# Normalising a block by token halves in a single-core transformer stack

## The reference, cut to what matters

```
def _rmsnorm(x, g):
    x32 = x.astype(jnp.float32)
    y = x32 * lax.rsqrt(jnp.mean(x32 * x32, axis=-1, keepdims=True) + RMS_EPS)
    return (y * g.astype(jnp.float32)).astype(x.dtype)
...
        u = _rmsnorm(h, norm_g[i, 0]) * (1 + sc1) + sh1
        h = h + MACARON_WEIGHT * g1 * _swiglu(u, ffn_w_gate[i, 0], ffn_w_up[i, 0], ffn_w_down[i, 0])
        u = _rmsnorm(h, norm_g[i, 1]) * (1 + sc2) + sh2
...
            mix = _hybrid_mixer(u, positions, hyb_w_in[j], fox_b_f[j], hyb_w_out[j])
...
            mix = _mla_mixer(u, positions, mla_w_down[j], mla_q_norm[j], mla_kv_norm[j],
                             mla_w_uq[j], mla_w_ukv[j], mla_w_out[j])
        h = h + g2 * mix
```

## Time and profile before

| | before |
|---|---|
| median of 3 runs | 3476.15 us |
| span of the profiled execution | 3472.8 us |
| around the span, against the median | 3.35 us |
| TensorE (PE) busy | 3406.4 us, 98% of the span |
| VectorE (DVE) busy | 2199.6 us, 63% |
| ScalarE (ACT) busy | 600.3 us, 17% |
| mean granted TensorE clock | 0.996 |

### The profile page before, as it was taken

How to read it: one execution, slowest core, us unless ns; L and a number is a source line. 1 busy time by engine, 2 the same in 40 slices (tenths; PEclk the granted TensorE clock), 3 DMA queues, 4 the chain that set the end, 5 groups by cost and what they waited for, 6 DMA issues and landing times.

```text
span 3472.8 us, 40732 instructions
## 1 busy us (share of the span) xinstructions
PE 3406.4 (98%) x16336; PEld 2811.9 (81%) x16336; DVE 2199.6 (63%) x4356; ACT 600.3 (17%) x1260; POOL 10.6 (0%) x12
## 2 busy tenths in 40 slices
PE   8999999999999999999999999999999999999999
PEld 6888867768888888888578888877688866888888
DVE  7776858767767677565356545554346567677754
ACT  2000023331000010001331000023411244012100
POOL 0000000000000000000000000010000000000000
PEclk9999999999999999999999999999999999999999
DMA  6433412213434434332112222222222211222222
GB/s 254 156 135 141 181 64 88 91 41 127 149 122 159 164 140 153 112 114 83 51 49 74 94 87 79 91 87 70 67 75 85 84 67 61 85 80 91 85 79 79
DMA packets 62083, 355.72 MB, mean 102 GB/s; under 512 B 6292, under 2 KB 15124, under 8 KB 32276
## 3 DMA queue, kind: packets, MB, share of 16 engines
q1 hardware_dynamic: 61895, 353.12, 29.2%
HBM read 350.83 MB, written 9.34 MB: 104 GB/s over the span
## 4 chain that ended last, share of the span: by engine, by line
PE 87%; DVE 9%; issue 2%; DMA 1%; ACT 1%; DVEq 0%; SPq 0%; ACTq 0%
PE turn L424 37%; PE lin L424 29%; PE lin L366 4%; PE lin L476 4%; PE turn L366 3%; PE score L1435 2%; PE out L1464 1%; PE lin L473 1%; DMA normed_T<-in_ada 1%; DVE work L823 1%; PE turn L1449 1%; PE out L424 1%; DVE work L2888 1%; DVE normed_sums L567 1%; PE turn L476 1%
## 5 line engine op out<-in xcount | busy, mean ns | idle before, releaser
L424 PE MATMUL turn<-normed_sums,weight_ring 128*128 128x256 f32 x3712 | 867.6, 379 | 0.4 <-DVE small L2907 0.4
L424 PEld LDWEIGHTS turn<-normed_sums,weight_ring 128*128 128x128 f32 x3712 | 705.0, 190 | 96.8 <-DVE small L2907 0.8
L424 PE MATMUL lin<-normed_T,weight_ring 128*128 128x256 f32 x2096 | 479.9, 380 | 1.2 <-ACT normed_T L779 1.2
L424 PEld LDWEIGHTS lin<-normed_T,weight_ring 128*128 128x128 f32 x2096 | 397.6, 190 | 58.8 <-issue 5.2
L503 DVE TENSOR_TENSOR products<-products,lin 128x512 f32<-128x512 f32 x182 | 125.1, 687 | 406.9 <-PE lin L424 378.8
L424 PE MATMUL turn<-arena,weight_ring 128*128 128x256 f32 x1618 | 371.3, 379 | 0.6 <-DVE arena L567 0.6
L424 PE MATMUL lin<-arena,weight_ring 128*128 128x256 f32 x1608 | 364.7, 380 | 2.0 <-DVE weight_ring L535 1.6
L424 PE MATMUL lin<-normed_sums,weight_ring 128*128 128x256 f32 x1432 | 345.5, 380 | 4.1 <-DVE normed_sums L567 4.1
L424 PEld LDWEIGHTS lin<-arena,weight_ring 128*128 128x128 f32 x1608 | 304.4, 190 | 45.8 <-DVE weight_ring L535 3.3
L424 PEld LDWEIGHTS turn<-arena,weight_ring 128*128 128x128 f32 x1618 | 306.6, 190 | 42.3 <-issue 1.0
L424 PEld LDWEIGHTS lin<-normed_sums,weight_ring 128*128 128x128 f32 x1432 | 270.9, 190 | 44.1 <-issue 6.2
(11 more groups left out here) (329 smaller groups left out, 3363.4 us busy)
## 6 DMA issues: line engine op xcount, KB each, us to landing
weight_ring<-in_up SPq DMA_DIRECT2D x110, 1024.0 KB, 4.8
arena<-in_ada SPq DMA_DIRECT2D x54, 768.0 KB, 4.4
weight_ring<-in_down SPq DMA_DIRECT2D x40, 1024.0 KB, 5.0
normed_T<-in_ada SPq DMA_DIRECT2D x36, 768.0 KB, 4.6
weight_ring<-in_down SPq DMA_DIRECT2D x20, 768.0 KB, 4.3
weight_ring<-in_dil_qk SPq DMA_DIRECT2D x9, 1024.0 KB, 5.0
weight_ring<-in_hyb_qk SPq DMA_DIRECT2D x8, 1024.0 KB, 4.8
weight_ring<-in_xbc SPq DMA_DIRECT2D x6, 1024.0 KB, 5.0
```

The costliest lines, as they stand in the source:

```text
L424: last = pe.matmul(o[:, n * H:(n + 1) * H], weight_block(slot, pairs, block, kp), op(kind, kp0 + kp), start=opens and n == 0 and kp == kps ...
```

## The change

Before, a norm treats all 512 tokens at once; after, it treats tokens 0 to 255 and then tokens 256 to 511. In the last slab of a stage the groups go a, b, c, e, d: c is now t3 alone, and d is t1 and b22, the two products that only the second token half needs. In a down projection this holds in the last chunk; the first two chunks close with d as well. The sums of squares, root, reciprocal and spread of the first half are issued between the calls of d (`first_half_norm_pe`, after its 3rd and 6th call). VectorE scales the first half tile by tile (`normed_dve`, 128x256 each), after two tiles of it adds the products of d to the residual (`late_adds_dve`, three instructions), and before tile 6 takes the second half's reciprocal. `arriving_pair_pe` takes two slabs together: b11 and b21 of slab 0, b11 and b21 of slab 1, then the other five products of slab 0 pair by pair, then t2 and the groups c and d of slab 1. The second half's sums follow its 5th call and the spread its 8th. VectorE then scales the second half and makes the operand sums in `second_half_dve`. `keep_busy` is no longer issued at norms. The hybrid mixer's first two projections run first on the first half, then on the second. The double norm issues its second spread after the 6th call of d and the 12th call of the pair. The output is stored in 16 halves instead of 8 tiles.

```diff
-        LAST_GROUPS = "abcde"
-        LAST_PRODUCTS = {"d": ((6, "b22"),), "e": ((3, "t4"),)}
+        LAST_GROUPS = "abce"
+        LAST_PRODUCTS = {"c": ((2, "t3"),), "e": ((3, "t4"),), "d": ((4, "t1"), (6, "b22"))}
...
+        PAIR_RINGS = ((0, 1, 0, 4), (2, 3, 4, 0), (1, 2, 3, 0))
+
+        def arriving_pair_pe(pe, c, op, beside):
+
+            there = halves_there(pe, c)
+            slots = [take_summed(pe, c), c.n["slab"] % SLOTS]
+            for n in range(2):
...
+                for kp in range(4):
+                    for o, block, kind in ((first, 0, "b11"), (second, 1, "b21")):
+                        there(kind, kp)
+                        last = pe.matmul(o, weight_block(slots[n], 4, block, kp), op(kind, kp), start=kp == 0, stop=kp == 3,
+                                         skip_group_check=True)
...
+                        beside()
...
+            for kp in range(4):
+                for g, n, block, kind in (("b", 1, 5, "t2"), ("c", 0, 4, "t1"), ("c", 1, 2, "t3"), ("d", 0, 6, "b22"),
+                                          ("d", 1, 3, "t4")):
+                    weights_there(pe, c, block, kp)
+                    there(kind, kp)
...
+            take_summed(pe, c)
+            c.banks(*PAIR_RINGS[1])
+            job_done(c)
+            for kp in range(4):
+                weights_there(pe, c, 5, kp)
+                last = pe.matmul(lin[3][:, H:T], weight_block(slots[1], 4, 5, kp), op("t2", kp), start=False, stop=kp == 3,
+                                 skip_group_check=True)
+            bank_close(c, last)
+            for g in "cd":
+                product_group(pe, c, slots[1], 4, g, op)
...
-        def tail_sums_pe(pe, c, final=False):
-            for n in range(1, 4):
-                tail_sum_pe(pe, c, n, final)
+        def first_half_norm_pe(pe, c, final=False):
...
+                if i == 3:
+                    tail_sum_pe(pe, c, 1, final)
+                elif final and i == 6:
+                    second_spread_pe(pe, 0)
+                elif not final and i == 6:
+                    spread_half_pe(pe, c, 0)
...
-            spread_pe(pe, c)
-            if not final:
-                keep_busy(pe, score[0], 3)
+        def second_half_norm_pe(pe, c):
...
+                if i == 5:
+                    second_half_sums_pe(pe, c)
+                elif i == 8:
+                    spread_half_pe(pe, c, 1)
...
+        def late_adds_dve(v, c, inst):
+
+            b = c["late_bank"]
+            o = lin[b]
+            v.wait_ge(lin_full[b], c[f"bank{b}"])
+            v.wait_ge(dve_step, c["late"])
+            add_to_tail(v, inst, 7, 1, o[:, 0:H]).then_inc(tail_ready, 1)
+            vlink(v, c, add_to_tail(v, inst, 6, 1, o[:, 0:H]))
+            add_to_tail(v, inst, 6, 1, o[:, H:T]).then_inc(lin_taken[b], 1)
...
-        def normed_dve(v, c, scale_tile, ahead=4):
-
-            rinv_dve(v, c)
-            rinv_there(v, c)
+        LATE_ADDS = {"slab": 2, "chunks": 2}
+        LATE_ROOT = {"slab": 6, "chunks": 6}
+
+        def normed_dve(v, c, prev, scale_half, ahead=4):
+
+            what, inst, sums_ahead = prev
+            reciprocal_dve(v, c, 0)
+            if sums_ahead:
+                weight_sums(v, c, 3)
+            half_there(v, c)
+            for k in range(KT + 1):
+                if k == LATE_ADDS[what]:
+                    late_adds_dve(v, c, inst)
+                if k == LATE_ROOT[what]:
+                    reciprocal_dve(v, c, 1)
+                if k < KT:
+                    scale_half(0, k)
+            half_there(v, c)
+            second_half_dve(v, c, lambda k: scale_half(1, k), ahead)
+
+        def second_half_dve(v, c, scale_tile, ahead):
+            c.add("u", KT)
             for k in range(ahead):
                 scale_tile(k)
...
+        def normed_act(s, c, prev, shift_half=lambda h, k: None, first_copy=True):
+
+            what = prev[0]
+            for k in range(KT + 1):
+                if k == LATE_ADDS[what]:
+                    late_squares_act(s, c)
+                if k == LATE_ROOT[what]:
+                    root_act(s, c, 1)
+                if k < KT:
+                    shift_half(0, k)
+            if first_copy:
+                c.banks(*PAIR_RINGS[0])
+                product_step_act(s, c, "a")
+            for k in range(KT):
+                shift_half(1, k)
...
-                    for n, g in enumerate(LAST_GROUPS if m == 3 else GROUPS):
-                        if (m, ch, g) == (3, 2, "d"):
+                    for g in (LAST_GROUPS + "d"[:ch < 2] if m == 3 else GROUPS):
+                        n = "abcd".find(g)
+                        if (m, ch, g) == (3, 2, "c"):
...
+            beside = first_half_norm_pe(pe, c, final)
+            product_group(pe, c, slot, 3, "d", hidden_op, kp0=8, opens=False, last_slab=True, beside=beside)
...
+                for n in range(2 * KT):
+                    h, k = divmod(n, KT)
+                    e.wait_ge(result_ready, n + 1)
+                    e.dma_start(out[k][:, h * H:(h + 1) * H], half(A[:, k, :], h)).then_inc(result_stored, 16)
```

More of the change, by code:

```diff
@@ L587, in tiles_seen, with halves_there, there, halves_seen @@
             c.add("sums", 3 * KT // 2)
+        def halves_there(pe, c):
+            tiles0, sums0 = c["u"], c["sums"]
+            def there(kind, kp):
+                if kind in ("b11", "b21"):
+                    pe.wait_ge(u_ready, tiles0 + 2 * kp + (1 if kind == "b11" else 2))
+                elif kind != "b22":
+                    pe.wait_ge(sums_made, sums0 + 3 * kp + {"t1": 1, "t3": 1, "t2": 2, "t4": 3}[kind])
+            return there
+        def halves_seen(c):
+            c.add("u", 2 * KT)
+            c.add("sums", 3 * KT // 2)
         u_pairs = in_pairs(uT)
@@ L631, in spread_half, with rinv_half, spread_half_pe @@
             return ins
+        rinv_bank = (outp[1], outp[0])
+        def rinv_half(h):
+            return rinv_bank[h][:, 0:H]
+        def spread_half_pe(pe, c, h):
+            c.add("spread")
+            pe.wait_ge(rinv_ready, c["spread"])
+            for b in range(2):
+                ins = pe.transpose(rinv_bank[h][:, b * P:(b + 1) * P], roots[h][:, b:b + 1].to_broadcast([P, P]), C("ident"))
+            ins.then_inc(rinv_spread, 1)
         def spread_pe(pe, c):
@@ L670, in tail_act, with late_squares_act, add_to_tail, sums @@
                 product_step_act(s, c, g)
[L671 to L678, removed]
-        def tail_dve(v, c, inst, ahead=True):
[L682 to L689, removed]
+            for n in range(2):
+                c.add("tail")
+                s.wait_ge(tail_ready, c["tail"])
+                tail_square_act(s, c, n, final)
+            root_act(s, c, 0)
+        def late_squares_act(s, c, final=False):
+            c.add("tail")
+            s.wait_ge(tail_ready, c["tail"])
+            tail_square_act(s, c, 2, final)
+            c.wait_mark(s, "blocks")
+            tail_square_act(s, c, 3, final)
+        def add_to_tail(v, inst, m, h, src):
+            tile = half(hT[:, m, :], h)
+            if inst is None:
+                return v.tensor_tensor(tile, src, tile, ALU.add)
+            return v.scalar_tensor_tensor(out=tile, in0=src, scalar=gate[:, inst, m:m + 1], in1=tile, op0=ALU.mult,
+                                          op1=ALU.add)
+        def tail_dve(v, c, inst, ahead=True):
+            def sums(stage):
                 if ahead:
-                    for stage in stages:
-                        weight_sums(v, c, stage)
+                    weight_sums(v, c, stage)
             job_done(c, note="p1_there")
@@ L775, in ada_norm_act, with ada_norm_dve, shift_half @@
+        def ada_norm_dve(v, c, inst, prev):
+            normed_dve(v, c, prev, lambda h, k: v.scalar_tensor_tensor(
+                out=half(uT[:, k, :], h), in0=half(hT[:, k, :], h), scalar=gs[:, inst, k:k + 1], in1=rinv_half(h),
+                op0=ALU.mult, op1=ALU.mult).then_inc(scaled, 1))
+        def ada_norm_act(s, c, inst, prev, first_copy=True):
             layer, sub = inst // 3, inst % 3
-            for k in range(KT):
+            def shift_half(h, k):
                 c.add("scaled")
@@ L1161, in tail_sp @@
         def tail_sp(c, s):
[L1162 to L1164 removed]
+            skip_jobs(c, 3)
+            job_done(c, slot=s)
         def out_pe(pe, c, op, there, begun=""):
@@ new lines, in second_half_renorm_pe, with beside @@
+        def second_half_renorm_pe(pe, c):
+            done = itertools.count(1)
+            def beside():
+                i = next(done)
+                if i == 5:
+                    second_half_sums_pe(pe, c, True)
+                elif i == 12:
+                    second_spread_pe(pe, 1)
+                elif i == 16:
+                    for h in range(2):
+                        c.add("spread")
+                        pe.wait_ge(rinv_ready, c["spread"])
+                        spread_half(pe, score[1], h, roots).then_inc(rinv_spread, 1)
```

(1 more changed line is left out.)

352 lines of the change are left out of this document (228 added, 124 removed).

## The result

The changed kernel takes 3501.26 us (median, 3498.22 to 3503.94) against 3475.56 us of the kernel before on the same chip: ratio 1.0073, 95% interval 1.006 to 1.0085. Forecast were 3490.4 us and a range of 3477 to 3503. The direction is as forecast and the time lies in the range, near its upper end. A loss of 14.2 us was forecast; the medians are 25.7 apart and the two profiled spans 24.5.

What follows compares the result with a forecast made beforehand. TensorE, busy 98% of the span, was taken to set the time. Six norms +13.9 us, hybrid 0, last norm +0.3 gave +14.2: span 3487.0, time 3490.4 us, range 3477 to 3503.

Steps and rivals of the forecast that it cites:

- First half's chain and first tiles: Start of FFN 1's norm: d's calls hide the chain; tile 0 at 4.67 us after e, TensorE waits 0.5.
- Late adds and second root: First half of FFN 1's norm: TensorE waits 1.4 us at tile 2 and 1.4 more at tile 6.
- the lower bound: Waits at adds and root smaller by up to 1.5 us a norm if adds overlap more: -9; range's low end 3481.
- The operand sums: Second half of FFN 1's norm on VectorE: well covered, 0.15 us of waiting counted.
- After a chunk: Norms after a chunk: 8.6 us each, waits 1.35 at tile 0 and 1.2 at tile 2; FFN 2 +2.5, latent attention +2.4.
- theory A: Follow-up expectation that waits at tiles 2 and 6 go: late adds alone 3490 to 3497 us, with early weight sums 3462 to 3472.
- Slab 1's weight sums: Made while slab 0 is combined: 1.73 us of calls cover 4.33, so TensorE waits 2.6 at slab 1's t2; the deciding step.
- My rival "faster": Cover works, early waits vanish: 3464 us, or 3448 with slab 1's weight sums also in time (16 more); chance 0.10.
- The mis-sized term: Dilated attention's norm, as a chunk (2.4) with stage 3 ending later: +3.4 us; its small root instructions priced as covered.
- The clock rival: Clock falls to 1.2 GHz in all six norms: 6 x 1.7 = 10 us more, up to 3503; chance 0.15.
- The likeliest case alone: Whole kernel slower by 5 to 22 us, without clock or even case: 3481 to 3498 us; chance 0.63.
- Hybrid and last norm: Hybrid's norm 6.8 against 6.76 us, so 0; last norm to the end 11.1 against 10.82, +0.3.

Runs made afterwards that it cites:

- the run with early weight sums and bank 3: Changed kernel with slab 1's weight sums ahead of the second half's reciprocal and the last slab's group d in bank 3, not 0: 3476.15 us.
- the runs with the late adds: Changed kernel with late adds and second root moved after the eighth half tile: alone 3521.2 us, with slab 1's weight sums also made early 3499.05 us.
- the last version: Changed kernel with early weight sums, group d in bank 3 and two idle products at each place in the norms' waits: 3474.23 us, ratio 0.9995.

## Why the prediction was right, and which term was mis-sized

**First half's chain and first tiles.** Right: d hides the chain, and there is no idle time between e and the end of d. The first call came at 4.62 in FFN 1 (4.67 forecast).

**Late adds and second root.** Right in mechanism, and VectorE's idle time ahead of the second reciprocal was 2.10 us (about 2 forecast). The waits were 0.98 and 0.93, by the forecast's count 1.21 and 1.18; 1.4 each was forecast. It isn't that the adds overlap more, as the lower bound had it: from their start to the next tile is 1.31, as forecast.

```profile
805.62 1.40 DVE L811 SCALAR_TENSOR_TENSOR residual_T<-turn,residual_gates,residual_T 128x256 f32<-128x256 f32 x3
806.93 1.65 DVE L950 SCALAR_TENSOR_TENSOR normed_T<-residual_T,norm_scales,out 128x256 f32<-128x256 f32 x4
```

They start 4.32 after e; with tile 2 forecast at 6.94, less 1.15 and 1.31, they would have started at 4.48. And tile 2 takes 1.07 from its scaling to TensorE's call, not 1.15. The operand sums cost nothing (0.15 forecast), so VectorE's second half never held TensorE at slab 0's t2.

**After a chunk** the sum was right (8.43, forecast 8.6) for a wrong reason. I placed 1.35 ahead of tile 0 and 1.2 ahead of tile 2; in FFN 2 and the latent attention it was one wait of 2.3 for a bank. I had not followed the ring of banks through the last slab. In the change it cost nothing beyond what tile 2 would have cost, which the run with early weight sums and bank 3 shows. In the runs with the late adds it was 4.67 three times; they missed theory A by 24 and 27 us, 19 of them shown to be the bank's.

**Slab 1's weight sums.** Right in place and size: 2.54 us (2.6 forecast) five times, 4.52 in the dilated attention (4.74, from 2.6 and the 2.14 by which stage 3 ends later there). Early weight sums take all of it out, and with it nearly the whole loss. My rival "faster" priced weight sums done in time at 16 us; it gave 23 between the medians, 17.2 of them the waits.

**The mis-sized term** is the dilated attention: +3.4 forecast, +8.5 measured in the first profile, 2.9 more behind its t2. I had priced its norm at full clock. At full clock the path was right: with idle products in its waits the stretch of 31.12 leaves 12.98, +3.5 against the kernel before. The clock rival spoke of waits at t2 in all six stages at 1.7 each; what came was two falls in one stage (5.0 and 2.9) in one profile, and smaller ones in more stages in the other (the dilated stretch there is +5.2). Forecast and clock rival were not two cases but one: the waits that I forecast can carry a clock loss with them, some 8 us in the first profile and 11 in the second. The likeliest case alone (3481 to 3498) missed; that the time still lay in the range is owed to the clock rival, which I had given 0.15 and which set the upper end. That this stage waits long ahead of its first tile (1.97 us) could have been seen in the code: in it the late adds stand ahead of all eight half tiles.

The Trainium skill, TensorE: Matmul & The Clock Gate, section on HAM oscillation, tells of a kernel in which the waits between groups of matmuls return the engine to half clock each time. The runs agree for the wait of 4.52 us (three times of three, with the kernel with late adds alone) and for the kernel without idle products (the rows above), and not always for the 2.54 us at t2: none of five in the first profile, three of five in each of the other three that have these waits.

**Hybrid and last norm.** For the hybrid 0 was forecast; the traces of before and after are 0.5 us apart ahead of it and 0.5 behind it. For the last norm +0.3 was forecast, +0.9 measured.

**Open:** why the clock falls behind a given wait in one run and not in the next, and why the sums' stretch lasted 10 us in one profile and 4 in the other.

## What to carry to other kernels

When work is moved to give one chain cover, list whose cover it was: eight calls moved ahead here left 1.73 us of cover for 4.33 us of weight sums. A wait of TensorE can cost more than its length, so price it with a share for the clock. Idle products in the waits were worth 13 us to the kernel before; in the last version they held the clock in the norms, but no gain is shown. They must fit (two of 0.43 us in a wait of 0.9). Follow the banks of a ring through a reordering as well as the operands: a wait can be for the place, and a fix that moves the reader then makes it longer.

## What the runs showed of the hardware that was not expected

While GpSimd copies, VectorE's adds of two SBUF buffers take longer here, and those with an operand in a PSUM bank don't. VectorE's timeline at the end of slab 0 of the dilated attention in after:

```profile
2285.84 0.69 DVE L564 TENSOR_TENSOR products<-products,lin 128x512 f32<-128x512 f32 x1
2286.44 0.98 DVE L589 TENSOR_TENSOR weight_ring<-weight_ring 128x512 f32<-128x512 f32 x1
2287.34 1.56 DVE L590 TENSOR_TENSOR weight_ring<-weight_ring 128x512 f32<-128x512 f32 x1
2288.83 0.68 DVE L570 TENSOR_TENSOR products<-products,lin 128x512 f32<-128x512 f32 x1
```

GpSimd's in the same time:

```profile
2285.75 8.15 POOL L2737 COPY arena<-normed_T 128x512 f32<-128x512 f32 x6 [2285.31 <-DVE small L2517]
```

The same weight sums take 0.68 us each in FFN 1. The four take 2.0 us more in all here, which is why this stage's wait at t2 is 4.52 and not 2.54. The Trainium skill, GPSIMD Engine Reference, section Specifications, says that GpSimd shares its way to the buffers with VectorE, with contention for instructions that have two inputs there; the rows agree, 0.98 to 1.56 against 0.68.
